# Weight differences of the next unit at products three and four, and token sums begun between the last two row turns

## Chip, cores and metric

The kernel runs on one core of one Trainium2 chip. The metric is the device time of one execution in microseconds. Before the change the median of 3 runs is 3083.6 us (3083.21 to 3086.71).

## What is computed

Two blocks of layers on 512 tokens of width 1024, all in float32. The part that matters here is the gated feed-forward layer, which the second block runs four times, named (l, i) for layer l and place i:

```
def swiglu(x, w_gu, w_down):
    g, u = jnp.split(x @ w_gu, 2, axis=-1)
    return (jax.nn.silu(g) * u) @ w_down

for layer in range(2):
    x = layer_norm(ALPHA * x + 0.5 * swiglu(x, w_gu[layer, 0], w_down[layer, 0]), ...)
    x = layer_norm(ALPHA * x + mixer(x) @ w_out[layer], ...)
    x = layer_norm(ALPHA * x + 0.5 * swiglu(x, w_gu[layer, 1], w_down[layer, 1]), ...)
```

The inner width is 2816: w_gu is 1024 x 5632, w_down is 2816 x 1024.

## The kernel before, in words

**Split operands.** Every product is made from a high part (rounded by a copy on ScalarE) and a low part (the difference to it, a subtraction on VectorE). One 128x128 product is three matmuls: high by high, high by low, low by high (L665 to L667). So each operand costs one ScalarE copy ("high") and one VectorE subtraction ("low"), in that order.

**Units.** The 2816 columns are 11 units of 256. Unit 0 (panels "first") is an ordinary product; each of the units 1 to 10 takes its gate and its up columns by one level of a Strassen-Winograd scheme with FACTORS = 7 products, numbered 0 to 6. A product is 24 matmuls 256 columns wide. Its stationary side is a *factor* of the weights: products 0 and 1 take quarters of the gate panel as they are, product 5 one of the up panel; products 3, 2, 4 and 6 take weight *differences*, which VectorE makes with `difference(u, n)` for n = 3 (L2298), 2 (L2302), 4 (L2304) and 6 (L2308), called d3, d2, d4 and d6 here. Its moving side is the tokens, or one of four token *sums* (sum 1 to 4) made once for each layer by `token_sum(n)` on VectorE (L2265 to L2279), then split by `sum_high` and `sum_low`. Product 2 takes sum 2, product 3 sum 1, product 4 sum 3, product 5 sum 4.

**Buffers.** Two raw panels of 1 MB (RAW[0], RAW[1], "raw" in the rows): the gate panel of a unit in one, the up panel in the other. d3 and d4 are written over raw, d2 into `difference`, d6 into `xt_spare`. Factors go into a ring of 5 slots (w_high, w_low and unit_slot in the rows), so factor q+5 may be written when product q is done.

**Order of the work.** Each engine runs its own list, written by hand as a loop over q (product n of unit u), in order:

- SyncE loads panels in order. The gate panel of unit u+1 waits until factor (u, 3) is ready and d6 of unit u is made; the up panel waits for factor (u, 5).
- ScalarE at step (u, n): copy the bank that product n left ("snapshot", L1753; for products 0, 2, 3 and 4), at n = 2 and 6 a silu, then `high(q + 5)` (L1713): it waits for the panel (n = 0, 1, 5) or the difference.
- VectorE at step (u, n): at n = 1 add for the gate (L2349, `gate_summed`), at n = 5 and 6 the adds and products of the hidden values (L2352 to L2360); at n = 4 d3 and d2 of unit u+1, at n = 6 d4 of unit u+1; then `low(q + 5)` (L2255); at n = 0, after it, d6 of the unit itself. d3 first waits until the up panel has landed.
- TensorE, product n of unit u: waits for its factor, and for n = 2, 4, 5 and 6 until the snapshot of product n-2 is taken:

```
if n in (2, 4, 5, 6):
    pe.wait_ge(sem["snapped"], at("snapped", (f, u, n - 2)))
```

**Ahead of a feed-forward layer** stands `rows(s, y)`: it forms the normed rows tile by tile (4 tiles of 128 tokens), TensorE turns them, ScalarE and VectorE write the high part XTH (L1463) and the low part XTL (L1918) of the turned tokens, and `xt_ready` is given for each tile. The product of unit 0 runs between and behind the turns (`edge_product`); it needs tile 3 only for its second half. Layer (1, 0) has no such turns directly ahead: the key and value products lie between.

## Time and profile before

| What | Value |
|---|---|
| median of 3 runs | 3083.6 us |
| the profiled execution's own time | 3080.08 us |
| its span | 3077.9 us |
| TensorE busy (matmul) | 2904.7 us, 94% |
| TensorE weight loads busy | 2544.3 us, 83% |
| VectorE busy | 1719.4 us, 56% |
| ScalarE busy | 1258.2 us, 41% |
| DMA mean | 91 GB/s |
| mean granted TensorE clock | 0.983 of full |

The profiled execution lies 2.2 us above its span and 3.5 us below the median. TensorE's matmuls are pipelined, so the record of one is longer than the distance to the next; a stretch without a wait shows as fully busy. The page's mean clock hides short stretches at the lower level (0.5 in these units, 1.2 instead of 2.4 GHz). The four unit loops lie at 1074 to 1320 us (0, 0), 1645 to 1891 (0, 1), 2083 to 2334 (1, 0) and 2706 to 2950 (1, 1).

### The profile page before, as it was taken

What the parts mean: (1) busy time and instruction counts of PE and PEld (TensorE: products, weight loads), DVE (VectorE), ACT (ScalarE), POOL (GpSimd) and SP (SyncE); (2) the same over time, 40 slices, a digit from 0 to 9 for tenths busy, and PEclk for the clock granted to TensorE, in tenths of its full rate; (3) what the DMA queues carried; (4) which work ended last, traced back from release to release, by engine and by line L of the source; (5) the groups of instructions that cost most, each with busy time, mean ns of one, the idle gap of its engine ahead of it and who ended that gap; (6) DMA issues with size and microseconds to landing.
All of it is one profiled execution on the core that took longest, in us unless ns stands there. A gap on an engine that the chain in (4) does not pass through costs nothing.

```text
span 3077.9 us, 43267 instructions
## 1 busy us (share of the span) xinstructions
PE 2904.7 (94%) x18236; PEld 2544.3 (83%) x18236; DVE 1719.4 (56%) x2263; ACT 1258.2 (41%) x2081; POOL 101.7 (3%) x153
## 2 busy tenths in 40 slices
PE   7999999999999988899998889997999999989998
PEld 6888887788887878888778888887988876889987
DVE  3464343333336776744668666357665458586653
ACT  3324234444444334433653444224443248444431
POOL 1000000020000000000000000010000011000000
PEclk9999999999999999999999999998999999999999
DMA  5332222222222222233122223351323330212322
GB/s 199 126 109 96 96 96 83 83 77 89 76 79 78 82 83 83 83 123 100 56 69 73 93 83 110 103 146 56 103 89 107 86 97 1 81 57 91 102 103 76
DMA packets 186257, 278.67 MB, mean 91 GB/s; under 512 B 29578, under 2 KB 127034, under 8 KB 185936
## 3 DMA queue, kind: packets, MB, share of 16 engines
q1 hardware_dynamic: 177024, 247.17, 24.8%
q0 software_dynamic: 9040, 28.73, 2.9%
q8 instruction: 145, 2.38, 0.3%
q14 instruction: 48, 0.39, 0.0%
HBM read 271.56 MB, written 4.25 MB: 90 GB/s over the span
## 4 chain that ended last, share of the span: by engine, by line
PE 67%; DVE 15%; issue 7%; ACT 5%; DMA 4%; POOL 0%; SPq 0%; DVEq 0%; ACTq 0%; POOLq 0%
PE bank L665 18%; PE bank L667 18%; PE bank L666 18%; DMA raw<-in_ffn_w_gu 4%; DVE difference L2302 2%; DVE raw L2298 2%; PE bank L803 2%; DVE raw L2304 2%; ACT snapshot L1753 1%; PE bank L891 1%; ACT w_high L1713 1%; PE bank L859 1%; ACT w_low L1713 1%; PE bank L875 1%; PE bank L823 1%
## 5 line engine op out<-in xcount | busy, mean ns | idle before, releaser
L1900 DVE TENSOR_TENSOR w_low<-raw,w_high 128x2048 fp32r<-128x2048 f32 (+1 forms) x132 | 296.1, 2243 | 664.0 <-ACT w_high L1451 658.2
L1451 ACT ACTIVATE w_high<-raw 128x2048 fp32r<-128x2048 f32 (+1 forms) x132 | 247.3, 1874 | 528.3 <-PE bank L667 520.4
L665 PE MATMUL bank<-xt_high,w_high 128*128 128x512 f32 (+1 forms) x1128 | 408.0, 362 | 3.5 <-DVE w_high L2255 2.8
L666 PE MATMUL bank<-xt_low,w_high 128*128 128x512 f32 (+1 forms) x1128 | 399.4, 354 | 0.0
L667 PE MATMUL bank<-xt_high,w_low 128*128 128x512 f32 (+1 forms) x1128 | 399.1, 354 | 0.0
L665 PE MATMUL bank<-w_high,hidden_high 128*128 128x512 f32 x640 | 249.3, 390 | 0.0
L667 PE MATMUL bank<-w_high,hidden_low 128*128 128x512 f32 x640 | 249.0, 389 | 0.0
L666 PE MATMUL bank<-w_low,hidden_high 128*128 128x512 f32 x640 | 249.0, 389 | 0.0
L665 PEld LDWEIGHTS bank<-xt_high,w_high 128*128 128x128 f32 x1128 | 213.7, 189 | 40.4 <-issue 12.5
L667 PEld LDWEIGHTS bank<-xt_high,w_low 128*128 128x128 f32 x1128 | 212.7, 189 | 31.2
L666 PEld LDWEIGHTS bank<-xt_low,w_high 128*128 128x128 f32 x1128 | 213.9, 190 | 27.2
L665 PE MATMUL bank<-sum_high,w_low 128*128 128x256 f32 x512 | 152.8, 298 | 39.9 <-ACT snapshot L1753 39.9
L665 PE MATMUL bank<-sum_high,w_high 128*128 128x256 f32 x512 | 150.6, 294 | 31.6 <-ACT snapshot L1753 30.2
L667 PE MATMUL bank<-sum_high,w_low 128*128 128x256 f32 x512 | 151.1, 295 | 0.0
L666 PE MATMUL bank<-sum_low,w_low 128*128 128x256 f32 x512 | 151.0, 295 | 0.0
L2255 DVE TENSOR_TENSOR w_low<-raw,w_low 128x1024 fp32r<-128x1024 f32 x80 | 98.0, 1225 | 93.8 <-ACT w_low L1713 91.1
L2255 DVE TENSOR_TENSOR w_high<-raw,w_high 128x1024 fp32r<-128x1024 f32 x80 | 98.0, 1225 | 90.3 <-ACT w_high L1713 88.0
L666 PE MATMUL bank<-sum_low,w_high 128*128 128x256 f32 x512 | 148.3, 290 | 0.0
L667 PE MATMUL bank<-sum_high,w_high 128*128 128x256 f32 x512 | 148.2, 289 | 0.0
L666 PEld LDWEIGHTS bank<-w_low,hidden_high 128*128 128x128 f32 x640 | 120.2, 188 | 24.9
L665 PEld LDWEIGHTS bank<-sum_high,w_low 128*128 128x128 f32 x512 | 104.2, 204 | 44.1 <-issue 43.9
L667 PEld LDWEIGHTS bank<-w_high,hidden_low 128*128 128x128 f32 x640 | 120.1, 188 | 24.9
(448 smaller groups left out, 7208.1 us busy)
## 6 DMA issues: line engine op xcount, KB each, us to landing
raw<-in_ffn_w_gu SPq DMA_DIRECT2D x80, 1024.0 KB, 5.8
raw<-in_ffn_w_down SPq DMA_DIRECT2D x44, 1024.0 KB, 4.9
raw<-in_b_w_in SPq DMA_DIRECT2D x40, 1024.0 KB, 5.0
raw<-in_a_w_in SPq DMA_DIRECT2D x24, 1024.0 KB, 5.1
raw<-in_a_w_out SPq DMA_DIRECT2D x8, 1024.0 KB, 4.9
raw<-in_ffn_w_gu SPq DMA_DIRECT2D x16, 512.0 KB, 5.2
raw<-in_w_out SPq DMA_DIRECT2D x5, 1024.0 KB, 4.8
raw<-in_w_mem_kv SPq DMA_DIRECT2D x4, 1024.0 KB, 5.4
```

What stands on the lines that cost most here:

```text
L665: pe.matmul(o, lh, rh, start=start, stop=False, skip_group_check=True)
L666: pe.matmul(o, lh, rl, start=False, stop=False, skip_group_check=True)
L667: return pe.matmul(o, ll, rh, start=False, stop=stop, skip_group_check=True)
L803: ins = pe.matmul(ps[4 + m % 2][:, a:b], q, k, start=True, stop=True)
L823: ins = pe.matmul(ps[7][half:half + 64, x * P:x * P + P], v, PTs[m % 4][:, a:a + P], start=start, stop=stop)
L1451: act.activation(homes[n][0][:, 0:w], RAW[n % 2][:, 0:w], ACT.Copy).then_inc(sem["w_high_ready"], step("w_high_ready", n))
L1713: act.activation(dst, src, ACT.Copy).then_inc(sem["factor_high"], step("factor_high", (f, u, n)))
L1900: dve.tensor_tensor(homes[n][1][:, 0:w], RAW[n % 2][:, 0:w], homes[n][0][:, 0:w].bitcast(F32), ALU.subtract).then_inc(sem["w_low_ready"], ...
L2255: dve.tensor_tensor(dst, src, high.bitcast(F32), ALU.subtract).then_inc(sem["factor_ready"], step("factor_ready", key))
L2298: ins = dve.tensor_tensor(b11, b12, b11, ALU.subtract)
L2302: ins = dve.tensor_tensor(t2, b22, b11, ALU.subtract)
L2304: ins = dve.tensor_tensor(b12, b22, b12, ALU.subtract)
```

## The change

1. **Weight differences.** On VectorE d3 and d2 of unit u+1 move from step n = 4 to n = 3; d6 and d4 of unit u+1 are both made at n = 4, d6 first (before: d4 at n = 6 of unit u, d6 at n = 0 of unit u+1, after that step's low part). Unit 1 keeps d6 at the end of step 0.
2. **Token sums.** Sum 3 and sum 4 begin as high + low of a quarter of the tokens (`join_quarters`), which needs tiles 0 and 1 only. Sum 1 is made in two halves of 128 tokens (`sum_half`), the first of which needs tile 2. In three of the four layers both joins stand between the last rows and the low part of tile 2, and the first half between the low parts of tiles 2 and 3. Sum 2 is then one subtraction (before 2), sum 4 one more (before 3), sum 3 two more (before 3).
3. **First unit.** ScalarE copies sums 1, 2 and 4 ahead of the silus of unit 0. VectorE makes sum 4 ahead of the factors, the low part of factor 2 ahead of the hidden values of unit 0, and at step 0 also the gate's add (before: step 1) and the low part of sum 4 (before: step 1), ahead of factor 5 and d6. `high(5)` stands ahead of sum 3 on ScalarE.

The diff (calls of `rows` left out: those ahead of (0, 0), (0, 1) and (1, 1) get the layer's name as `sums`):

```diff
@@ -1725,16 +1725,17 @@
             high(1)
 
             def sum_high(n):
-                act.wait_ge(sem["sum_ready"], at("sum_ready", (f, n)))
+                act.wait_ge(sem["sum_ready"], at("sum_ready", (f, 1, 1) if n == 1 else (f, n)))
                 act.activation(tiles["sum_high"][n][:], tiles["sum"][n][:],
                                ACT.Copy).then_inc(sem["sum_high"], step("sum_high", (f, n)))
 
+            sum_high(1)
             sum_high(2)
+            sum_high(4)
             for j in range(2):
                 act.wait_ge(sem["product_done"], at("product_done", ("acc", ("first", l, i), j)))
                 act.activation(SNAP[j][:].rearrange("p a n -> p (a n)"), ps[j][:], ACT.Silu).then_inc(sem["gate_read"], step("gate_read", (f, j)))
             high(2)
-            sum_high(1)
             high(3)
             for q in range(count):
                 u, n = 1 + q // FACTORS, q % FACTORS
@@ -1758,13 +1759,11 @@
                 if n == 6:
                     act.activation(GATE2[:].rearrange("p a n -> p (a n)"), A[:],
                                    ACT.Silu).then_inc(sem["unit_gated"], step("unit_gated", (f, u, 1)))
+                if q + 5 < count:
+                    high(q + 5)
                 if q == 0:
                     sum_high(3)
                     high(4)
-                if q == 1:
-                    sum_high(4)
-                if q + 5 < count:
-                    high(q + 5)
                 if u == UNITS - 1:
                     if n == 2:
                         hidden_high(0)
...
@@ -2022,8 +2021,32 @@
             end(2)
             begin(3)
             end(3)
+            if sums:
+                join_quarters(sums, s)
             low(2)
+            if sums:
+                sum_half(sums, s, 0)
             low(3)
+
+        def token_part(high, k0, t0, n=256):
+            return (XTH if high else XTL)[:, k0:k0 + 4, t0:t0 + n].bitcast(F32)
+
+        def join_quarters(f, s):
+
+            dve.wait_ge(sem["xt_ready"], at("xt_ready", (s, 1)))
+            for n, k0 in ((3, 0), (4, 4)):
+                dve.tensor_tensor(FFN[f]["sum"][n][:], token_part(True, k0, 0), token_part(False, k0, 0),
+                                  ALU.add).then_inc(sem["quarter_joined"], step("quarter_joined", (f, n)))
+
+        def sum_half(f, s, h):
+
+            dve.wait_ge(sem["xt_ready"], at("xt_ready", (s, 2 + h)))
+            t0 = 256 + P * h
+            out = FFN[f]["sum"][1][:, :, P * h:P * h + P]
+            link(dve.tensor_tensor(out, token_part(True, 0, t0, P), token_part(True, 4, t0, P), ALU.add))
+            link(dve.tensor_tensor(out, out, token_part(False, 0, t0, P), ALU.add))
+            ins = dve.tensor_tensor(out, out, token_part(False, 4, t0, P), ALU.add)
+            ins.then_inc(sem["sum_ready"], step("sum_ready", (f, 1, h)))
 
         def attend_slot(name, s):
 
@@ -2255,30 +2278,21 @@
                 dve.tensor_tensor(dst, src, high.bitcast(F32),
                                   ALU.subtract).then_inc(sem["factor_ready"], step("factor_ready", key))
 
-            def x(high, k0, t0):
-                return (XTH if high else XTL)[:, k0:k0 + 4, t0:t0 + 256].bitcast(F32)
-
             def token_sum(n):
 
                 out = tiles["sum"][n][:]
-                if n == 1:
-                    link(dve.tensor_tensor(out, x(True, 0, 256), x(True, 4, 256), ALU.add))
-                    link(dve.tensor_tensor(out, out, x(False, 0, 256), ALU.add))
-                    ins = dve.tensor_tensor(out, out, x(False, 4, 256), ALU.add)
                 if n == 2:
-                    link(dve.tensor_tensor(out, tiles["sum"][1][:], x(True, 0, 0), ALU.subtract))
-                    ins = dve.tensor_tensor(out, out, x(False, 0, 0), ALU.subtract)
+                    dve.wait_ge(sem["quarter_joined"], at("quarter_joined", (f, 3)))
+                    dve.wait_ge(sem["sum_ready"], at("sum_ready", (f, 1, 1)))
+                    ins = dve.tensor_tensor(out, tiles["sum"][1][:], tiles["sum"][3][:], ALU.subtract)
+                if n == 4:
+                    dve.wait_ge(sem["quarter_joined"], at("quarter_joined", (f, 4)))
+                    dve.wait_ge(sem["sum_ready"], at("sum_ready", (f, 2)))
+                    ins = dve.tensor_tensor(out, out, tiles["sum"][2][:], ALU.subtract)
                 if n == 3:
-                    link(dve.tensor_tensor(out, x(True, 0, 0), x(True, 0, 256), ALU.subtract))
-                    link(dve.tensor_tensor(out, out, x(False, 0, 0), ALU.add))
-                    ins = dve.tensor_tensor(out, out, x(False, 0, 256), ALU.subtract)
-                if n == 4:
-                    high, low2 = tiles["sum_high"][2][:].bitcast(F32), tiles["sum_low"][2][:].bitcast(F32)
-                    link(dve.tensor_tensor(out, x(True, 4, 0), high, ALU.subtract))
-                    link(dve.tensor_tensor(out, out, x(False, 4, 0), ALU.add))
-                    ins = dve.tensor_tensor(out, out, low2, ALU.subtract)
+                    link(dve.tensor_tensor(out, out, token_part(True, 0, 256), ALU.subtract))
+                    ins = dve.tensor_tensor(out, out, token_part(False, 0, 256), ALU.subtract)
                 ins.then_inc(sem["sum_ready"], step("sum_ready", (f, n)))
-                dve.wait_ge(sem["sum_ready"], at("sum_ready", (f, n)))
 
             def sum_low(n):
                 dve.wait_ge(sem["sum_high"], at("sum_high", (f, n)))
@@ -2315,14 +2329,18 @@
                                   ALU.subtract).then_inc(sem["hidden_split"], step("hidden_split", (f, u)))
 
             prepare(ids["first", l, i][-1])
-            dve.wait_ge(sem["xt_ready"], at("xt_ready", (s, TT - 1)))
-            token_sum(1)
+            if f == (1, 0):
+                join_quarters(f, s)
+                sum_half(f, s, 0)
+            sum_half(f, s, 1)
             token_sum(2)
+            token_sum(4)
             low(0)
             low(1)
             difference(1, 3)
             difference(1, 2)
             sum_low(2)
+            low(2)
             for j in range(2):
                 dve.wait_ge(sem["product_done"], at("product_done", ("acc", ("first", l, i), 2 + j)))
                 dve.wait_ge(sem["gate_read"], at("gate_read", (f, j)))
@@ -2330,10 +2348,9 @@
                 dve.tensor_tensor(tiles["hidden"][0][:, j, :], ps[2 + j][:], SNAP[j][:].rearrange("p a n -> p (a n)"),
                                   ALU.mult).then_inc(sem["up_read"], step("up_read", *labels))
             dve.wait_ge(sem["up_read"], at("up_read", (f, 1)))
-            low(2)
+            token_sum(3)
             sum_low(1)
             low(3)
-            token_sum(3)
             difference(1, 4)
             for q in range(count):
                 u, n = 1 + q // FACTORS, q % FACTORS
@@ -2342,11 +2359,16 @@
                 def bank(b):
                     return b[:].rearrange("p (a n) -> p a n", a=2)
 
-                if n in (1, 5):
-                    dve.wait_ge(sem["unit_done"], at("unit_done", (f, u, n)))
-                if n == 1:
+                def gate_sum():
+
+                    dve.wait_ge(sem["unit_done"], at("unit_done", (f, u, 1)))
                     dve.wait_ge(sem["snapped"], at("snapped", (f, u, 0)))
                     dve.tensor_tensor(SNAP[0][:], bank(B), SNAP[0][:], ALU.add).then_inc(sem["gate_summed"], step("gate_summed", (f, u)))
+
+                if n == 5:
+                    dve.wait_ge(sem["unit_done"], at("unit_done", (f, u, n)))
+                if n == 1 and u > 1:
+                    gate_sum()
                 if n == 5:
                     dve.wait_ge(sem["snapped"], at("snapped", (f, u, 2)))
                     link(dve.tensor_tensor(SNAP[1][:], bank(C), SNAP[1][:], ALU.add))
@@ -2362,20 +2384,19 @@
                 if q == 0:
                     sum_low(3)
                     low(4)
-                    token_sum(4)
-                if q == 1:
+                    gate_sum()
                     sum_low(4)
-                if n == 4 and u + 1 < UNITS:
+                if n == 3 and u + 1 < UNITS:
                     difference(u + 1, 3)
                     difference(u + 1, 2)
-                if n == 6 and u + 1 < UNITS:
+                if n == 4 and u + 1 < UNITS:
+                    difference(u + 1, 6)
                     difference(u + 1, 4)
                 if q + 5 < count:
                     low(q + 5)
-                if n == 0:
-                    if u == 1:
-                        dve.wait_ge(sem["product_done"], at("product_done", ("panel", ids["first", l, i][1])))
-                    difference(u, 6)
+                if q == 0:
+                    dve.wait_ge(sem["product_done"], at("product_done", ("panel", ids["first", l, i][1])))
+                    difference(1, 6)
                 if u == UNITS - 1:
                     if n == 2:
                         hidden_low(0)
...
```

How the lists of VectorE move, at three places. First the turn from one unit to the next, here with unit 3 (L2255 and L2278 are the low parts of factors, L2298, L2302, L2304, L2308 before and L2312, L2316, L2318, L2322 now are d3, d2, d4, d6; numbers behind a name tell buffers apart). Before, on VectorE:

```order
L2298 TENSOR_TENSOR raw_61<-raw_62,raw_61 128x1024
L2302 TENSOR_TENSOR difference_82<-raw_62,raw_61 128x1024
L2255 TENSOR_TENSOR w_low_65<-difference_82,w_low_65 128x1024
L2352 TENSOR_TENSOR snapshot_258<-bank,snapshot_258 128x512
L2354 TENSOR_TENSOR hidden_00_85<-snapshot_258,snapshot_257 128x2x256
L2357 TENSOR_TENSOR snapshot_259<-snapshot_259,snapshot_260 128x512
L2255 TENSOR_TENSOR w_high_64<-raw_61,w_high_64 128x1024
L2360 TENSOR_TENSOR hidden_00_85<-snapshot_259,gate_late 128x2x256
L2304 TENSOR_TENSOR raw_62<-raw_62 128x1024
L2255 TENSOR_TENSOR w_low_66<-raw_62,w_low_66 128x1024
L2255 TENSOR_TENSOR unit_slot_81<-raw_62,unit_slot_81 128x1024
L2308 TENSOR_TENSOR xt_spare_54<-raw_61,difference_82 128x4x256
```

Now, on VectorE at the same place:

```order
L2312 TENSOR_TENSOR raw_61<-raw_62,raw_61 128x1024
L2316 TENSOR_TENSOR difference_82<-raw_62,raw_61 128x1024
L2278 TENSOR_TENSOR w_high_63<-raw_61,w_high_63 128x1024
L2322 TENSOR_TENSOR xt_spare_54<-raw_61,difference_82 128x4x256
L2318 TENSOR_TENSOR raw_62<-raw_62 128x1024
L2278 TENSOR_TENSOR w_low_65<-difference_82,w_low_65 128x1024
L2374 TENSOR_TENSOR snapshot_258<-bank,snapshot_258 128x512
L2376 TENSOR_TENSOR hidden_00_85<-snapshot_258,snapshot_257 128x2x256
L2379 TENSOR_TENSOR snapshot_259<-snapshot_259,snapshot_260 128x512
L2278 TENSOR_TENSOR w_high_64<-raw_61,w_high_64 128x1024
L2382 TENSOR_TENSOR hidden_00_85<-snapshot_259,gate_late 128x2x256
L2278 TENSOR_TENSOR w_low_66<-raw_62,w_low_66 128x1024
```

d6 and d4 now stand directly behind the low part of factor 1, ahead of that of factor 2; d4 no longer stands behind the hidden values, nor d6 at the end.

Second, the last row turns of layer (0, 0) and the start of its feed-forward part (L1918 and L1917 are the low part of the turned tokens; sum_00_74, 71, 77 and 80 are sums 1, 2, 3 and 4). Before, on VectorE:

```order
L1992 TENSOR_TENSOR x_rows<-x_rows,xt_spare_54 128x1024
L1918 TENSOR_TENSOR xt_low<-bank,xt_high 128x4x128 x4
L2265 TENSOR_TENSOR sum_00_74<-xt_high 128x1024
L2266 TENSOR_TENSOR sum_00_74<-sum_00_74,xt_low 128x1024
L2267 TENSOR_TENSOR sum_00_74<-sum_00_74,xt_low 128x1024
L2269 TENSOR_TENSOR sum_00_71<-sum_00_74,xt_high 128x1024
L2270 TENSOR_TENSOR sum_00_71<-sum_00_71,xt_low 128x1024
L2255 TENSOR_TENSOR w_high_63<-raw_61,w_high_63 128x1024
L2255 TENSOR_TENSOR w_low_65<-raw_61,w_low_65 128x1024
L2298 TENSOR_TENSOR raw_61<-raw_62,raw_61 128x1024
L2302 TENSOR_TENSOR difference_82<-raw_62,raw_61 128x1024
L2285 TENSOR_TENSOR sum_low_70<-sum_00_71,sum_high_69 128x1024
```

Now, on VectorE at the same place:

```order
L1991 TENSOR_TENSOR x_rows<-x_rows,xt_spare_54 128x1024
L2038 TENSOR_TENSOR sum_00_77<-xt_high,xt_low 128x1024
L2038 TENSOR_TENSOR sum_00_80<-xt_high,xt_low 128x1024
L1917 TENSOR_TENSOR xt_low<-bank,xt_high 128x4x128 x2
L2046 TENSOR_TENSOR sum_00_74<-xt_high 128x4x128
L2047 TENSOR_TENSOR sum_00_74<-sum_00_74,xt_low 128x4x128
L2048 TENSOR_TENSOR sum_00_74<-sum_00_74,xt_low 128x4x128
L1917 TENSOR_TENSOR xt_low<-bank,xt_high 128x4x128 x2
L2046 TENSOR_TENSOR sum_00_74<-xt_high 128x4x128
L2047 TENSOR_TENSOR sum_00_74<-sum_00_74,xt_low 128x4x128
L2048 TENSOR_TENSOR sum_00_74<-sum_00_74,xt_low 128x4x128
L2287 TENSOR_TENSOR sum_00_71<-sum_00_74,sum_00_77 128x1024
```

The two joins stand ahead of the low part of tile 2 and three adds of half width ahead of that of tile 3.

Third, the first unit of (0, 0), from d4 on. Before, on VectorE:

```order
L2304 TENSOR_TENSOR raw_62<-raw_62 128x1024
L2285 TENSOR_TENSOR sum_low_76<-sum_00_77,sum_high_75 128x1024
L2255 TENSOR_TENSOR unit_slot_81<-raw_62,unit_slot_81 128x1024
L2277 TENSOR_TENSOR sum_00_80<-xt_high,sum_high_69 128x1024
L2278 TENSOR_TENSOR sum_00_80<-sum_00_80,xt_low 128x1024
L2279 TENSOR_TENSOR sum_00_80<-sum_00_80,sum_low_70 128x1024
L2255 TENSOR_TENSOR w_high_63<-raw_62,w_high_63 128x1024
L2308 TENSOR_TENSOR xt_spare_54<-raw_61,difference_82 128x4x256
L2349 TENSOR_TENSOR snapshot_257<-bank,snapshot_257 128x512
L2285 TENSOR_TENSOR sum_low_79<-sum_00_80,sum_high_78 128x1024
```

Now, on VectorE at the same place:

```order
L2318 TENSOR_TENSOR raw_62<-raw_62 128x1024
L2299 TENSOR_TENSOR sum_low_76<-sum_00_77,sum_high_75 128x1024
L2278 TENSOR_TENSOR unit_slot_81<-raw_62,unit_slot_81 128x1024
L2366 TENSOR_TENSOR snapshot_257<-bank,snapshot_257 128x512
L2299 TENSOR_TENSOR sum_low_79<-sum_00_80,sum_high_78 128x1024
L2278 TENSOR_TENSOR w_high_63<-raw_62,w_high_63 128x1024
L2322 TENSOR_TENSOR xt_spare_54<-raw_61,difference_82 128x4x256
L2278 TENSOR_TENSOR w_low_65<-xt_spare_54,w_low_65 128x1024
```

The three subtractions for sum 4 are gone from here; the gate's add and the low part of sum 4 now stand ahead of d6.

## Rows read from the trace of the kernel before

**Rows 1.** Waits of TensorE, whole run: who waited for whom, us in total, times, longest.
```profile
PE bank L665 <- ACT snapshot L1753: 128.3, 61, 11.2
```

**Rows 2.** Windows: stretch, length, busy us of each engine (instructions), PEclk, DMA share, GB/s.
```profile
1099.38:1320.29 220.91, 194.30 (x1560) 191.16 (x1561) 153.85 (x150) 96.47 (x122) 0.00 (x0) 0.98 0.27 89
1670.79:1890.90 220.11, 194.21 (x1561) 191.16 (x1561) 153.84 (x150) 96.48 (x122) 0.00 (x0) 0.98 0.27 88
2112.80:2333.66 220.86, 200.81 (x1561) 198.52 (x1562) 155.38 (x152) 97.02 (x122) 0.00 (x0) 0.95 0.28 91
2731.86:2949.88 218.02, 199.44 (x1562) 197.15 (x1562) 153.86 (x150) 96.91 (x122) 0.00 (x0) 0.95 0.28 89
1154.70:1160.46 5.76, 5.76 (x50) 5.71 (x48) 5.69 (x7) 1.16 (x2) 0.00 (x0) 1.00 0.00 0
```

**Rows 3.** Timeline of VectorE, units 5 and 6: start us, us, [idle before <-releaser].
```profile
1188.28 1.22 DVE L2308 TENSOR_TENSOR xt_spare<-raw,difference 128x1024 f32<-128x1024 f32 x1
1196.07 1.22 DVE L2255 TENSOR_TENSOR w_high<-raw,w_high 128x1024 fp32r<-128x1024 f32 x1 [4.21 <-ACT w_high L1713]
1198.64 1.22 DVE L2298 TENSOR_TENSOR raw<-raw,raw 128x1024 f32<-128x1024 f32 x1
1199.90 1.23 DVE L2302 TENSOR_TENSOR difference<-raw,raw 128x1024 f32<-128x1024 f32 x1
1202.32 1.23 DVE L2255 TENSOR_TENSOR w_high<-difference,w_high 128x1024 fp32r<-128x1024 f32 x1 [1.20 <-ACT w_high L1713]
1205.51 1.23 DVE L2255 TENSOR_TENSOR w_low<-raw,w_low 128x1024 fp32r<-128x1024 f32 x1
1207.25 1.22 DVE L2304 TENSOR_TENSOR raw<-raw 128x1024 f32<-128x1024 f32 x1
1211.03 1.23 DVE L2255 TENSOR_TENSOR w_high<-raw,w_high 128x1024 fp32r<-128x1024 f32 x1
1212.17 1.22 DVE L2308 TENSOR_TENSOR xt_spare<-raw,difference 128x1024 f32<-128x1024 f32 x1
```

**Rows 4.** Timeline of ScalarE in the same stretch.
```profile
1194.98 1.06 ACT L1713 ACTIVATE w_high<-raw 128x1024 fp32r<-128x1024 f32 x1 [3.38 <-DMA raw<-in_ffn_w_gu]
...
1208.51 1.06 ACT L1713 ACTIVATE unit_slot<-raw 128x1024 fp32r<-128x1024 f32 x1 [4.85 <-DVE raw L2304]
```

**Rows 5.** Timeline of TensorE in the same stretch.
```profile
1196.66 0.36 PE L665 MATMUL bank<-sum_high,w_low 128*128 128x256 f32 x1 [1.49 <-ACT snapshot L1753]
...
1210.19 0.36 PE L665 MATMUL bank<-sum_high,w_high 128*128 128x256 f32 x1 [1.78 <-ACT snapshot L1753]
```

**Rows 6.** Timeline of VectorE, row turns and first unit of (0,0).
```profile
1057.04 1.29 DVE L1918 TENSOR_TENSOR xt_low<-bank,xt_high 128x512 fp32r<-128x512 f32 x2 [2.51 <-ACT xt_high L1463]
1060.78 1.29 DVE L1918 TENSOR_TENSOR xt_low<-bank,xt_high 128x512 fp32r<-128x512 f32 x2 [2.45 <-ACT xt_high L1463]
...
1068.40 1.23 DVE L2255 TENSOR_TENSOR w_high<-raw,w_high 128x1024 fp32r<-128x1024 f32 x1
...
1091.28 1.22 DVE L2308 TENSOR_TENSOR xt_spare<-raw,difference 128x1024 f32<-128x1024 f32 x1
```

**Rows 7.** Timeline of VectorE, row turns ahead of (0,1).
```profile
1626.26 1.29 DVE L2003 SCALAR_TENSOR_TENSOR x_rows<-x_rows,small,gain 128x1024 f32<-128x1024 f32 x1 [0.67 <-POOL small L2580]
1628.27 1.29 DVE L1918 TENSOR_TENSOR xt_low<-bank,xt_high 128x512 fp32r<-128x512 f32 x2 [0.73 <-ACT xt_high L1463]
1632.01 1.29 DVE L1918 TENSOR_TENSOR xt_low<-bank,xt_high 128x512 fp32r<-128x512 f32 x2 [2.45 <-ACT xt_high L1463]
```

**Rows 8.** Timeline of VectorE, first unit of (1,0).
```profile
2081.74 1.23 DVE L2255 TENSOR_TENSOR w_high<-raw,w_high 128x1024 fp32r<-128x1024 f32 x1 [18.83 <-ACT w_high L1713]
...
2104.63 1.22 DVE L2308 TENSOR_TENSOR xt_spare<-raw,difference 128x1024 f32<-128x1024 f32 x1
```

**Rows 9.** Timeline of VectorE in (1,0): both panels asked for after the first row.
```profile
2128.35 1.22 DVE L2308 TENSOR_TENSOR xt_spare<-raw,difference 128x1024 f32<-128x1024 f32 x1
...
2139.00 1.23 DVE L2298 TENSOR_TENSOR raw<-raw,raw 128x1024 f32<-128x1024 f32 x1 [0.40 <-DMA raw<-in_ffn_w_gu]
```

10 lines of the change are left out of this document (5 added, 5 removed).

## Prediction

> **What bounds the kernel now.** I read three views in this order. First the waits of TensorE: nearly all its idle time is one line, 128.3 us in 61 waits [rows 1], all inside the unit loops of the four feed-forward layers. The releaser named, the snapshot, need not be the cause: it is the last link of a longer chain. Second, windows over each loop from product 5 of unit 1 to the start of the down product, 65 products each: 220.91, 220.11, 220.86 and 218.02 us, together 879.90 [rows 2]. The last window holds two products without a wait: 5.76 us for 48 matmuls, 0.12 us a matmul, so 2.88 a product and 20.16 us a unit. 65 products need 187.2 us, four loops 748.8. Thus 131.1 us lie there in waits and in matmuls at the lower clock. The clock belongs in it: the last two loops have a mean granted clock of 0.95 and fewer waits than the first two at 0.98, with nearly the same length [rows 2], as they would if something other than TensorE set the pace.
>
> Third, the timelines show what. On VectorE d6 of unit 5 starts at 1188.28 and d6 of unit 6 at 1212.17: a turn of 23.89 us against TensorE's 20.16 [rows 3]. The turn is one closed chain. d6 frees the raw gate panel; the next one lands and ScalarE takes it at 1194.98, 5.5 us after d6 ended [rows 4]; the low part follows at 1196.07, a second one, d3 at 1198.64, d2, then 1.20 us of waiting for ScalarE's copy of d2, the hidden values, d4 at 1207.25, again a wait for ScalarE's copy, the low part of factor 5 and d6 [rows 3]. TensorE waits twice in a turn, though no factor is late. ScalarE's next snapshot is queued behind a copy. For product 5 (1.49 us [rows 5]) that is the copy waiting for the panel, for product 2 (1.78 us) the copy waiting 4.85 us for d4 [rows 4].
>
> **The unit loop after the change.** d6 of unit u+1 is now made at product 4 of unit u, so the gate panel is held by the low part of factor 3 alone. I follow the new turn from the landing of the up panel, which d3 needs, with distances from rows 3:
> - d3 to d2 1.26, d2 to low part 1 1.25 (d2 is waited for), low part to d6 1.14 (as 1211.03 to 1212.17), d6 to d4 and d4 to low part 2 1.25 each: 6.15.
> - Low part 2 to low part 3 with the hidden values between, 1202.32 to 1205.51: 3.19.
> - Low part 3 to 4: the slot that d4 has today, 1205.51 to 1207.25: 1.74. Low part 4 to 5: 1.14. Low part 5 itself: 1.23, and the up panel is asked for.
>
> That is 13.45 us. ScalarE's copies of d2 and d4 are now covered by d6 and other low parts. To it comes the transfer. Where both panels are asked for together, at the end of d6 at 2129.57, d3 waits until 2139.00: the second lands 9.4 us after [rows 9]. The gate panel is now asked for 1.74 + 1.14 = 2.9 us earlier than the up panel, which then lands 6.5 us after its own request, if the pair still takes 9.4. The turn is 13.45 + 6.5 = 19.95 us, under 20.16. Thus TensorE becomes the bound, narrowly. A small overshoot costs little: when unit 2 begins, VectorE is by my ledger some 2 us ahead of product 2, and only what adds up over eight turns beyond that is paid.
>
> ScalarE's snapshots: d4 is made before product 0, so the copy of factor 4 no longer holds the one for product 2. The gate panel is asked for at about the end of product 6, lands 5.5 us later, and its copy is due at the end of product 2, 3 × 2.88 = 8.6 us later: 3 us to spare. Both waits go; with no waits the clock stays up. What is late next is nothing on the list; VectorE's 13.45 us plus a panel is. The down product behind the loop waits for no copy that the change moves. I cost the loops at their 748.8 us: **−131.1**.
>
> The size of this term can be read in two ways. The rows show TensorE busy for 194.30 + 194.21 + 200.81 + 199.44 = 788.76 of the 879.90 us, which leaves 91.1 idle [rows 2]. By that column −91.1 would be all there is, and the end 2978 us. I take 131.1, since 48 matmuls in 5.76 us [rows 2] is a rate and slow matmuls count as busy. The Trainium skill's page "Perfetto Trace Analysis" (Identifying the Most-Contended Engine) says that the busy share of matmuls is not a good measure of the distance to the limit; by that rule the 2978 falls away.
>
> **The first unit.** Product 4 of unit 1 waits longest (up to 11.2 us [rows 1]): ScalarE's snapshot for it stands behind the copy of d6, and d6 behind all token sums on VectorE. After it the second gate panel is asked for, which fixes product 5. So both, and all behind, move with the end of d6. In (0, 0) VectorE runs without a pause from tile 3's low part to d6's end at 1092.50 [rows 6]. Linked full operations take 1.25 [rows 3]; those of half width I take at 0.72, from 1.29 for the pair in an xt_low row [rows 6] and a link. Removed: 11 sum operations, 13.75. Put in their place: three halves 2.16 and four full ones 5.0. Moved ahead of d6: the gate's add 0.61 and a low part 1.14. Together −13.75 + 7.16 + 1.75 = **−4.8**.
> The joins and the first half must hide in the row turns. In (0, 0) VectorE waits 2.51 and 2.45 us there [rows 6], against 2.4 for the joins and 2.1 for the half: free. Ahead of (0, 1) the first gap is 0.73 [rows 7]: joins from 1627.46 (1.2 after the rows' start) put tile 2's low part at 1629.74, and the half then puts tile 3's at 1633.11 instead of 1632.01. 1.1 us of d6's gain are lost, **−3.7**; TensorE may wait 0.7 us for tile 3, which costs nothing since product 4 waits for d6 anyway. (1, 1) has the same pattern: **−3.7**. In (1, 0) the sums are ready long before, VectorE waits 18.83 us for a copy [rows 8]; only sums 3 and 4 shorten the stretch (−5.0 + 1.75), and two copies more stand ahead of the silus, 1.9 us on ScalarE, of which low part 2 sees about 1.2: **−2.0**. Together −14.2.
>
> **Sum.** −131.1 − 14.2 = −145.3 against the profiled execution's 3080.1: 2934.8. The median lies 3.5 us higher; I predict **2938 us** for the median. Nothing is added elsewhere: transfers are the same in number and size, and VectorE's sums are 12 instructions a layer for 11, six of them of half width.
>
> **Rivals.**
> - *A, the panels set the pace.* The turn's margin is 0.2 us and rests on one distance. If the up panel lands 9.4 us after its own request (the longest wait rows show), the turn is 22.85. Eight turns of 2.7 too much, less 2 of advance, are 19.6 a layer, 78 in all: 3016. With 7.5 us the turn is 20.95, 4 a layer, 17 in all: 2955. For it: both panels share one queue. Against: a panel asked for alone is there in 5.5 [rows 3, 4], and the gate panel has a start of 2.9. Chance of A near its far end 0.10; its near end lies in the forecast's case. The Trainium skill's page "DMA: Bandwidth & Descriptors" (Bandwidth) has 1 MB occupy the engines for 6.15 us; an estimate by it is over 12 us for a pair and an end near A's. By that rule the trace does not agree: the pair took 9.4 in all [rows 9].
> - *B, it does only half of what it says.* The wait for product 5 stays because the gate panel's request, held by low part 3, is not early enough; only the wait for product 2 goes. 1.49 us over nine units and four layers are 54 us: 2992. Chance 0.06.
> - *C, slower.* d3 waits for the up panel, and it now stands one step earlier, ahead of d6, d4 and low parts 1 and 2 on VectorE's in-order list. From a landing more than 10.4 us after the request the turn exceeds today's 23.89. At 11.5 us each turn is 25.0, 1.1 × 36 = 40 us more, less 14: 3110. No row has such a landing. Chance 0.02. With it no change at all, 0.02.
>
> **Numbers.** Forecast 0.80, A 0.10, B 0.06, slower 0.02, same 0.02 (0.2%, 6 us, is about what a measurement of this kernel can tell from no change). The forecast's own bounds: the loops can give no more than their 131.1, and the first units give more only as d6 ends earlier; with my ledger of VectorE 4 us a layer too long the end is 2922. Upwards it reaches 2955 with late panels. The range goes on from there towards B, to the 2978 that the busy column gives: 2922 to 2978, with 0.20 left out. Faster 0.96.
>
> **What would show it.** Windows between the first units and the down products at 187 to 189 us each, clock 1.00 from unit 2 on; TensorE's waits fall from 128 to some 25 us, about 4 to 7 for each product 4 of unit 1 and some 2 for its product 5; VectorE's idle time before low part 5, released by ScalarE, which waits for TensorE; no wait of ScalarE for d4. d6 of unit 1 in (0, 0) ends near 1087.7. Wrong would be a turn of VectorE above 20.5 us with d3 released by the panel (A), or a wait of 1.2 to 1.5 us left before each product 5 (B).

## Result and profile after

| | Before | After |
|---|---|---|
| median | 3085.15 us (4 runs) | 2935.41 us (2934.14 to 2937.16, 4 runs) |
| the profiled execution's own time | 3080.08 us | 2937.16 us |
| its span | 3077.9 us | 2935.3 us |
| TensorE busy | 2904.7 us, 94% | 2866.2 us, 98% |
| mean granted clock | 0.983 | 0.994 |

The median before has one more run than at the time of the prediction. The ratio to the kernel before is 0.9514, 95% interval [0.9498, 0.9531]. The forecast was 2938 us for the median. Its sum, 2934.8 us for the profiled execution, is 2.4 us under the measured 2937.16.

The waits of TensorE, whole run, in the changed kernel: who waited for whom, us in total, times, longest.

```profile
PE bank L665 <- issue: 21.2, 8, 6.0
PE bank L784 <- DVE row L1938: 20.5, 6, 9.5
PE bank L665 <- DVE w_high L2278: 2.8, 1, 2.8
```

The 128.3 us for the snapshot [rows 1] are gone. Eight waits at the same line are left, now named "issue", all in unit 1. Four stand before product 4 (3.65, 3.76, 6.02 and 3.75 us) and three before product 5 (0.71, 1.26 and 0.68); these have the old cause under another name. The eighth, 1.35 us before product 2 of layer (1, 0), is new: there the kernel before had no wait. It costs nothing by itself, since product 4 of that layer waits for d6 anyway.

Windows over the four loops, from product 5 of unit 1 to the down product, against [rows 2] (columns as there).

```profile
1095.10:1282.57 187.47, 187.47 (x1560) 187.47 (x1561) 154.85 (x152) 99.41 (x122) 0.00 (x0) 1.00 0.33 107
1629.08:1816.34 187.26, 187.26 (x1561) 187.26 (x1561) 154.85 (x152) 99.79 (x122) 0.00 (x0) 1.00 0.33 107
2036.96:2224.23 187.27, 187.27 (x1560) 187.27 (x1561) 155.13 (x152) 99.55 (x122) 0.00 (x0) 1.00 0.33 107
2620.00:2807.27 187.27, 187.27 (x1560) 187.27 (x1561) 155.13 (x152) 99.56 (x122) 0.00 (x0) 1.00 0.33 107
```

The busy column of TensorE equals the length in each, and the clock is 1.00: no product waits. Together 749.27 us for 879.90, **130.6 us less**. The other 12.0 us of the span lie ahead of the loops: from one loop to the next product 5 the changed kernel is 4.3, 4.0, 1.3 and 2.4 us shorter, and behind the last loop nothing moved (128.02 and 128.03 us).

The timeline of VectorE in a settled stretch, from the end of one turn to the start of the next, against [rows 3].

```profile
1207.89 0.69 DVE L2366 TENSOR_TENSOR snapshot<-bank,snapshot 128x512 f32<-128x512 f32 x1
1209.05 1.23 DVE L2278 TENSOR_TENSOR w_low<-xt_spare,w_low 128x1024 fp32r<-128x1024 f32 x1 [0.46 <-ACT w_low L1713]
1212.87 1.22 DVE L2278 TENSOR_TENSOR unit_slot<-raw,unit_slot 128x1024 fp32r<-128x1024 f32 x1 [2.59 <-ACT unit_slot L1713]
1214.19 1.23 DVE L2312 TENSOR_TENSOR raw<-raw,raw 128x1024 f32<-128x1024 f32 x1
1215.45 1.22 DVE L2316 TENSOR_TENSOR difference<-raw,raw 128x1024 f32<-128x1024 f32 x1
1216.71 1.22 DVE L2278 TENSOR_TENSOR w_high<-raw,w_high 128x1024 fp32r<-128x1024 f32 x1
1217.86 1.22 DVE L2322 TENSOR_TENSOR xt_spare<-raw,difference 128x1024 f32<-128x1024 f32 x1
1219.11 1.23 DVE L2318 TENSOR_TENSOR raw<-raw 128x1024 f32<-128x1024 f32 x1
...
1234.36 1.23 DVE L2312 TENSOR_TENSOR raw<-raw,raw 128x1024 f32<-128x1024 f32 x1
```

d3 (L2312) comes 20.17 us after the one before, at TensorE's pace. In this stretch it waits for nothing; VectorE idles one step earlier, for ScalarE, whose copy waits until TensorE has freed a slot of the ring. That is what a kernel bound by TensorE looks like on VectorE.

The timeline of VectorE, ScalarE and TensorE in the first unit of (0, 0), against [rows 6].

```profile
1057.35 1.29 DVE L1917 TENSOR_TENSOR xt_low<-bank,xt_high 128x512 fp32r<-128x512 f32 x2 [0.24 <-ACT xt_high L1463]
1061.09 1.29 DVE L1917 TENSOR_TENSOR xt_low<-bank,xt_high 128x512 fp32r<-128x512 f32 x2 [0.27 <-ACT xt_high L1463]
...
1086.59 1.22 DVE L2322 TENSOR_TENSOR xt_spare<-raw,difference 128x1024 f32<-128x1024 f32 x1
```

```profile
1087.85 1.06 ACT L1713 ACTIVATE w_low<-xt_spare 128x1024 fp32r<-128x1024 f32 x1 [5.34 <-DVE xt_spare L2322]
1088.81 0.58 ACT L1754 ACTIVATE snapshot<-bank 128x512 f32<-128x512 f32 x1
```

```profile
1089.49 0.56 PE L665 MATMUL bank<-sum_high,unit_slot 128*128 128x256 f32 x1 [3.65 <-issue]
```

The waits of 2.51 and 2.45 us in the row turns are down to 0.24 and 0.27: joins and half sum fill them. d6 ends at 1087.81 (forecast 1087.7); its copy, the snapshot behind it and product 4 follow in a chain, as before.

### The profile page after: what moved, and what is told of

It is laid out like the page before. It is cut to its first block, busy times and chain, and to the rows that moved or that the text cites. A ratio compares the mean times of both kernels' runs of the same rounds, so it can differ in the third digit from the quotient of the medians.

```text
span 2935.3 us, 43271 instructions
## 1 busy us (share of the span) xinstructions
PE 2866.2 (98%) x18236; PEld 2515.3 (86%) x18236; DVE 1708.3 (58%) x2267; ACT 1269.1 (43%) x2081; POOL 101.4 (3%) x153
## 4 chain that ended last, share of the span: by engine, by line
PE 88%; DVE 7%; issue 2%; ACT 2%; DMA 1%; POOL 0%; SPq 0%; POOLq 0%; DVEq 0%; ACTq 0%
PE bank L665 25%; PE bank L667 25%; PE bank L666 25%; PE bank L803 2%; PE bank L891 1%; PE bank L859 1%; PE bank L875 1%; PE bank L823 1%; PE bank L812 1%; PE bank L676 1%; PE bank L679 1%; PE bank L678 1%; PE bank L784 1%; DVE sum_low L2299 1%; PE bank L1037 0%
## 5 line engine op out<-in xcount | busy, mean ns | idle before, releaser
L1754 ACT ACTIVATE snapshot<-bank 128x512 f32<-128x512 f32 x160 | 95.3, 596 | 182.3 <-PE bank L667 172.7
L665 PE MATMUL bank<-sum_high,w_high 128*128 128x256 f32 x512 | 145.4, 284 | 4.1 <-issue 4.0
L665 PE MATMUL bank<-sum_high,w_low 128*128 128x256 f32 x512 | 145.0, 283 | 0.9 <-DVE w_low L2278 0.9
L666 PE MATMUL bank<-sum_low,w_low 128*128 128x256 f32 x512 | 144.9, 283 | 0.0
L667 PE MATMUL bank<-sum_high,w_low 128*128 128x256 f32 x512 | 144.9, 283 | 0.0
L667 PE MATMUL bank<-sum_high,w_high 128*128 128x256 f32 x512 | 144.9, 283 | 0.0
L665 PEld LDWEIGHTS bank<-w_high,hidden_high 128*128 128x128 f32 x640 | 120.1, 188 | 24.8
L665 PE MATMUL bank<-w_high,xt_high 128*128 128x512 f32 (+1 forms) x336 | 130.2, 388 | 0.0
```

What stands on the lines that cost most here:

```text
L665: pe.matmul(o, lh, rh, start=start, stop=False, skip_group_check=True)
L666: pe.matmul(o, lh, rl, start=False, stop=False, skip_group_check=True)
L667: return pe.matmul(o, ll, rh, start=False, stop=stop, skip_group_check=True)
L1754: act.activation(SNAP[to][:].rearrange("p a n -> p (a n)"), bank[:], ACT.Copy).then_inc(sem["snapped"], step("snapped", (f, u, n)))
```

## Experiments

All kernels ran beside the kernel before on the same chip (its medians there were 3081.3 to 3083.8 us). "Window" is from product 5 of unit 1 to the down product.

### The two parts apart

`differences_alone` is the kernel before with this edit, `sums_alone` the changed kernel with its reverse:

```diff
-                if n == 4 and u + 1 < UNITS:
+                if n == 3 and u + 1 < UNITS:
                     difference(u + 1, 3)
                     difference(u + 1, 2)
-                if n == 6 and u + 1 < UNITS:
+                if n == 4 and u + 1 < UNITS:
+                    difference(u + 1, 6)
                     difference(u + 1, 4)
...
-                if n == 0:
+                if q == 0:
...
-                    difference(u, 6)
+                    difference(1, 6)
```

> The kernel before with the new places of the weight differences in the unit loop (d3, d2 at product 3; d6, d4 at product 4), token sums and first unit as they were. The turn theory (a closed chain over VectorE and the panels set 23.9 us a unit) gives the loops back whole, as in the changed kernel: about 130 us off 3085, so 2955, with the waits of up to 11 us at product 4 of unit 1 still there. A rival, that loops and sums help only together, would leave a turn above 20.5 us in this kernel and an end above 2975.

> The changed kernel with the weight differences at their old places; the token sums and the first unit as changed. The turn theory: windows of about 220 us between the first units and the down products as before, and only the first units' 12 us gained: 3073. If the late start of VectorE in the first unit was what kept the loop behind, the windows would be shorter too and the end under 3050.

Measured: `differences_alone` 2950.97 us, ratio 0.9577 [0.9563, 0.9592]; `sums_alone` 3067.21 us, ratio 0.9955 [0.994, 0.997]. That is 131.0 and 14.7 us less than before on their chip, 145.7 together; the whole change is worth 149.7 by its medians and 142.6 by the spans of the two profiled executions. Three of the four windows of `sums_alone`:

```profile
1095.32:1315.13 219.81, 196.37 (x1561) 193.65 (x1561) 154.00 (x150) 96.78 (x122) 0.00 (x0) 0.97 0.27 89
1661.59:1882.57 220.98, 199.95 (x1562) 197.16 (x1561) 153.80 (x150) 96.87 (x122) 0.00 (x0) 0.95 0.27 88
2102.16:2322.86 220.70, 192.61 (x1561) 189.60 (x1561) 154.09 (x150) 96.33 (x122) 0.00 (x0) 0.99 0.27 88
```

The fourth is 218.93 us long. The loops keep their length although their first units are as short as in the changed kernel. The parts do not need each other. These rows also show what the clock is worth here: at 0.99 and at 0.95 the window is 220.7 and 221.0 us. A faster TensorE only waits longer: in these windows its clock has no price of its own, since VectorE's turn sets the pace.

### d4 or d6 alone

```diff
                 if n == 4 and u + 1 < UNITS:
                     difference(u + 1, 3)
                     difference(u + 1, 2)
+                    difference(u + 1, 4)
```

This is `d4_early_alone` (d6 as before, at the end of step 0). In `d6_early_alone` the added line is `difference(u + 1, 6)`, and d4 stays at n == 6. Both have the token sums and the first unit of the changed kernel.

> The changed kernel, with d3, d2 and then d4 at product 4 and d6 at its old place, at the end of step 0 of its own unit. The turn theory: d4's own slot (1.25 us) and the wait for ScalarE's copy of it (1.2 us) leave the chain, but d6 still frees the gate panel, so the turn falls from 23.9 to about 21.4, the wait before product 5 stays, and the end is some 2985. The rival, that each wait of TensorE stands for itself, gives back just the 1.78 us before product 2, 64 us in all beside the 12: about 3009.

> The changed kernel, with d3, d2 and then d6 at product 4 and d4 at its old place, behind the hidden values of product 6. The turn theory: the gate panel is no longer freed by the last step of the chain, the turn of VectorE is about 20.0 us, so d4 is no longer late and the snapshot for product 2 comes in time although its place on ScalarE is the old one: 2935 to 2950. The rival, that each wait stands for itself, keeps the 1.78 us before product 2, 64 us: about 3000.

Measured: d4 early 2973.72 us, ratio 0.965 [0.9634, 0.9666]; d6 early 2952.32 us, ratio 0.9583 [0.9569, 0.9598]. One window of each (65 products):

```profile
1095.47:1292.83 197.36, 189.04 (x1561) 187.65 (x1561) 153.47 (x151) 96.22 (x122) 0.00 (x0) 1.00 0.30 99
```

```profile
1094.91:1286.16 191.25, 189.28 (x1561) 187.72 (x1561) 154.46 (x152) 97.87 (x122) 0.00 (x0) 1.00 0.32 105
```

With d4 early d3 comes every 21.42 us on average (1097.49 to 1268.83 in eight turns), as the turn theory had it (21.4). The end is 11 us under the expected 2985, which does not follow from that turn: (21.4 - 20.16) × 8 turns × 4 layers are 40 us on top of the changed kernel, 2975. The waits before product 2 are gone and one before product 5 is left in nearly each unit:

```profile
PE bank L665 <- ACT snapshot L1754: 28.8, 31, 2.6
```

With d6 early it comes every 20.39 us (1096.93 to 1260.04), 0.4 more than the ledger's 20.0, and the end is 2 us above the expected 2935 to 2950. Why the turn is 20.39 was not followed further. VectorE still waits 1.2 us a turn for ScalarE's copy of d4, but of that only some 0.2 us a unit reaches TensorE. The rival, that each wait is a loss by itself, wanted 3009 and 3000 and falls. The two gains overlap: the four windows add up to 786.3 us with d4 early (93.6 less than before), 767.9 with d6 early (112.0 less) and 749.3 with both (130.6 less). Either step shortens the same turn, and the second is worth only what is left above 20.16.

What d6 does in the old order shows on SyncE's queue. Its waits in the first window of the kernel before:

```profile
SPq L645 <- DVE xt_spare L2308: 205.8, 9, 24.3
SPq L654 <- DVE w_low L1900: 8.4, 1, 8.4
```

and in that of the changed kernel:

```profile
SPq L645 <- DVE xt_spare L2322: 97.8, 9, 12.3
SPq L654 <- DVE w_high L2278: 30.5, 7, 5.7
SPq L654 <- DVE w_low L2278: 27.6, 7, 5.7
SPq L654 <- DVE unit_slot L2278: 16.7, 4, 5.7
```

Before, the up panel's request never waited for a factor: each of the nine pairs was asked for at once when d6 was done. Now the gate panel goes when low part 3 is done and the up panel when low part 5 is, 18 waits of their own.

### d3 and d2 back at product 4

`d3_at_product_four`: in the changed kernel `difference(u + 1, 3)` and `difference(u + 1, 2)` stand at n == 4, ahead of d6 and d4.

> The changed kernel with all four differences at product 4, d3 and d2 one step later than in the change, behind the low part of factor 1. Now TensorE bounds the loop and VectorE waits some 3 us a turn, so one place costs nothing: 2935, within 5 us. The rival, that the move of d3 and d2 to product 3 carries part of the gain, gives windows over 190 us and an end above 2950.

Measured: 2935.6 us, ratio 0.952 [0.9504, 0.9536], the same as the change. Moving d3 and d2 to product 3 is worth nothing here: in either order VectorE waits in each turn for ScalarE's copies ahead of d3 (0.46 + 2.59 us in the changed kernel, 3.25 + 0.48 us in this one), and what is gained goes into these waits.

### How much margin the turn has

```diff
                 if n == 2:
...
+                    for again in range(2 if u > 1 else 0):
+                        link(dve.tensor_tensor(t2, b22, b11, ALU.subtract))
                     ins = dve.tensor_tensor(t2, b22, b11, ALU.subtract)
```

(`two_more_subtractions`; `one_more_subtraction` has range(1).)

> The changed kernel with d2 made twice in units 2 to 10, one more linked subtraction of 1.25 us on VectorE in each turn. In the changed kernel VectorE's own turn, where it still catches up, is 18.7 us (d3 of unit 4 at 1155.7, of unit 5 at 1174.4), so with one more it is 19.97, still under TensorE's 20.16: under 4 us more than 2935. By the prediction's ledger (19.95 without it) it would be 21.2, one us too long in each of eight turns: some 25 to 35 us more.

> The same with d2 made three times, two more linked subtractions in each turn. By the 18.7 us read from the changed kernel the turn is 21.2: 1.06 us too long over eight turns, less what VectorE is ahead by then (about 3 us), 5 to 8 us a layer, 20 to 30 us more than 2935. By the prediction's ledger (22.45) 2.3 too long, 16 to 18 a layer: about 65 to 75 more.

Measured: 2950.5 us with one (ratio 0.9569 [0.9554, 0.9583]), 15 more than the change; 2998.0 us with two (0.9724 [0.971, 0.9739]), 63 more. Both lie between the expectations: the margin is larger than the prediction's 0.2 us and smaller than the 1.4 that I read from one pair of rows of the changed kernel. The starts of d3 with two more subtractions, where VectorE sets the pace, show why:

```profile
1117.46 1.23 DVE L2312 TENSOR_TENSOR raw<-raw,raw 128x1024 f32<-128x1024 f32 x1 [0.66 <-DMA raw<-in_ffn_w_gu]
...
1140.20 1.23 DVE L2312 TENSOR_TENSOR raw<-raw,raw 128x1024 f32<-128x1024 f32 x1 [1.83 <-DMA raw<-in_ffn_w_gu]
...
1161.40 1.23 DVE L2312 TENSOR_TENSOR raw<-raw,raw 128x1024 f32<-128x1024 f32 x1 [0.63 <-DMA raw<-in_ffn_w_gu]
...
1182.62 1.23 DVE L2312 TENSOR_TENSOR raw<-raw,raw 128x1024 f32<-128x1024 f32 x1 [0.59 <-DMA raw<-in_ffn_w_gu]
...
1205.02 1.22 DVE L2312 TENSOR_TENSOR raw<-raw,raw 128x1024 f32<-128x1024 f32 x1 [1.83 <-DMA raw<-in_ffn_w_gu]
...
1226.27 1.22 DVE L2312 TENSOR_TENSOR raw<-raw,raw 128x1024 f32<-128x1024 f32 x1 [0.60 <-DMA raw<-in_ffn_w_gu]
```

The distances are 22.74, 21.20, 21.22, 22.40 and 21.25 us: in two of these five turns the up panel is 1.2 to 1.5 us late. Over the eight turns of this loop the mean is (1269.72 - 1096.16) / 8 = 21.70, over the four loops 21.84 (21.70, 21.88, 22.00 and 21.79); without the two additions (2.51) that is 19.3. With one more subtraction the mean of the four loops is 20.57, less 1.25 again 19.3. The margin of the changed kernel is thus 20.16 - 19.3 = **0.8 us a turn**. One more subtraction of 1.25 overruns it by 0.4, two by 1.7; in eight turns of four layers that is 13 and 54 us. The four windows are together 15.3 and 60.9 us longer than those of the changed kernel; the rest of 2 and 7 us was not followed further.

VectorE's idle time would have misled: it idles 3.3 us a turn in the changed kernel (0.22 + 0.46 + 2.59), and an addition of 1.25 still costs time. The chain runs through the landing of the up panel: VectorE may be idle there, but the chain is not.

### Sums behind the turns

`sums_behind_the_turns` leaves `join_quarters` and the first `sum_half` out of `rows` and puts them where (1, 0) has them, for all layers:

```diff
-            if sums:
-                join_quarters(sums, s)
             low(2)
-            if sums:
-                sum_half(sums, s, 0)
             low(3)
...
-            if f == (1, 0):
-                join_quarters(f, s)
-                sum_half(f, s, 0)
+            join_quarters(f, s)
+            sum_half(f, s, 0)
```

> The changed kernel with both joins and the first half of sum 1 behind the row turns in every layer, as it has them in (1, 0) alone; the work is the same. If they hid in the turns and d6 of unit 1 follows all of VectorE's list, d6 comes 4.6 us later in (0, 0) and 3.5 in (0, 1) and (1, 1): 11 to 12 us more than 2935. If product 4 of unit 1 does not hang on d6, under 3 more.

Measured: 2945.72 us, ratio 0.9553 [0.9539, 0.9567]; 10.3 more than the change. From the start of unit 1 to its product 5 the three layers take 25.11, 24.78 and 24.74 us instead of 20.94, 20.75 and 20.55; (1, 0), untouched, takes 27.37 and 27.82. The windows behind are the same to 0.3 us. So some 10 us of what sums and first unit give are the work hidden in the row turns.

### What the waits left in the first unit are worth

Waits of 3.7 to 6.0 us at product 4 and of up to 1.3 at product 5 are left, and the matmuls of product 4 behind such a wait run at a lower clock: granted 0.50 in (0, 0), 0.63, 0.67 and 0.66 in the other three layers. `snapshots_first` tries to take them by turning ScalarE's list in unit 1:

```diff
+                if q in (3, 4):
+                    high(q + 3)
-                if q + 5 < count:
+                if q + 5 < count and q not in (1, 2):
                     high(q + 5)
```

> The changed kernel with one piece of ScalarE's list turned in the first unit: the copy of d6 stands behind the snapshot of product 3, and the copies of factors 0 and 1 of unit 2 behind that of product 4; VectorE is untouched. If product 4 of unit 1 hangs on d6 only by ScalarE's order, its wait (3.7 us in three layers, 6.0 in (1, 0)) and that of product 5 go; what is late next is the low part of d2 of unit 2 on VectorE, ready at 1103.7 in (0, 0) where product 2 now starts at 1106.9: 3 us a layer, so some 2923. If the wait is VectorE's own (low part of factor 4 or of sum 3 late), nothing moves: 2935.

Measured: 2936.28 us, ratio 0.9533 [0.952, 0.9546]. The edit did not do what its expectation says: at q == 3 the copy of factor 1 of unit 2 came out ahead of the snapshot of product 4, so product 6 of unit 1 waits in its place, 3.2 us in (0, 0) (it starts at 1094.82; without the wait it would be 1091.45). `snapshots_first_again` has at q == 3 only the copy of d6, and at q == 4 those of factors 0 and 1 of unit 2.

> What the first of the two kernels with the snapshots first was meant to be: the copy of factor 1 of unit 2 too now stands behind the snapshot of product 4 (there it stood ahead, so that product 6 waited for the panel). Products 4, 5 and 6 of unit 1 should follow without a wait. But both earlier runs show the next link: the snapshot of product 0 of unit 2 overwrites what the hidden values of unit 1 read, and these stand behind six subtractions on VectorE, at 1105.0 in that run. So if VectorE's list is what counts, product 2 of unit 2 starts at about 1106.5 whatever TensorE saves before it: 2935, within 2 us. If the waits seen at products 4 and 5 were time lost in full, it would be some 2915.

Measured: 2937.62 us, ratio 0.9536 [0.9523, 0.9549]. In (0, 0) products 4, 5 and 6 of unit 1 follow without a wait and product 6 starts at 1091.72 instead of 1098.25, 6.5 us earlier. Waits before products 0, 1 and 2 of unit 2 (0.87, 1.24 and 2.62 us) and matmuls at the lower clock take nearly all of it back; product 2 starts 1.1 us earlier than in the changed kernel:

```profile
1105.77 0.38 PE L665 MATMUL bank<-sum_high,unit_slot 128*128 128x256 f32 x1 [2.62 <-ACT snapshot L1754]
```

On ScalarE that snapshot waited for the hidden values of unit 1 on VectorE, which stand behind d3, d2, d6, d4 and two low parts:

```profile
1105.02 0.60 ACT L1754 ACTIVATE snapshot<-bank 128x512 f32<-128x512 f32 x1 [1.59 <-DVE hidden L2381]
```

So the 6.5 us could not be had in this way: VectorE's list, not the wait that TensorE shows, fixes when unit 2 can go on. `d6_first_in_unit_one` therefore moves the work on VectorE:

```diff
                 if q == 0:
+                    dve.wait_ge(sem["product_done"], at("product_done", ("panel", ids["first", l, i][1])))
+                    difference(1, 6)
                     sum_low(3)
                     low(4)
...
+                if q == 3:
+                    high(7)
-                if q + 5 < count:
+                if q + 5 < count and q != 2:
                     high(q + 5)
```

> The changed kernel with d6 of unit 1 made directly behind d4 on VectorE, ahead of the low parts of sum 3 and factor 4, 5 us earlier, and on ScalarE the copy of factor 0 of unit 2 behind the snapshot of product 3. The gate panel of unit 2 is then asked for 5 us earlier and TensorE's waits at products 4 and 5 of unit 1 go; the low part of d2 of unit 2 comes at about 1101, one us late: 5 to 6 us a layer, so some 2913. If the up panel, asked for behind the low part of factor 5, is what fixes unit 2, it is no better than the kernel with the snapshots first, some 2923.

Measured: **2925.97 us** (2923.09 to 2926.24), ratio 0.9495 [0.9482, 0.9508], 10.3 less than `snapshots_first`, which ran beside it. In (0, 0) products 4 to 6 of unit 1 and 0 of unit 2 run without a wait, the latter at 1094.44 instead of 1101.13 (in (1, 0) product 4 still waits 1.65 us). Of these 6.7 us 2.6 are lost again before product 2 of unit 2 and 1.5 at the lower clock in it: some 2.5 us a layer are left of the 5 to 6 expected.

`hidden_values_early` goes after that wait: for unit 1 the hidden values of product 5 stand ahead of d3 and d2, and the low part of factor 2 of unit 2 ahead of d6 and d4.

```diff
-                if n == 5:
-                    dve.wait_ge(sem["unit_done"], at("unit_done", (f, u, n)))
...
-                if n == 5:
+                if q == 3 or n == 5 and u > 1:
+                    dve.wait_ge(sem["unit_done"], at("unit_done", (f, u, 5)))
...
+                if q == 4:
+                    low(9)
                 if n == 4 and u + 1 < UNITS:
```

> The kernel with d6 first in unit 1, and two more moves on VectorE for unit 1 alone: its hidden values of product 5 stand ahead of d3 and d2 of unit 2, in the 2.9 us in which d3 waits for the up panel, and the low part of factor 2 of unit 2 stands ahead of d6 and d4. If the snapshot that follows the hidden values is what held product 2 of unit 2 (2.6 us in each layer, then 1.5 us at the lower clock), both go and the next bound is the low part of factor 2 near 1099: 3 to 4 us a layer, some 2912. If that wait is the low part itself, under 4 us are gained: 2922 or more.

Measured: 2924.9 us (2922.02 to 2925.62), ratio 0.9489 [0.9476, 0.9502], not to be told from the kernel before it. The expectation's first theory, 2912, is wrong; the number fits the second, but not for its reason, since the wait is still the snapshot's and not the low part's. ScalarE's rows show the link that took over:

```profile
1101.14 1.06 ACT L1713 ACTIVATE w_low<-raw 128x1024 fp32r<-128x1024 f32 x1 [2.30 <-DVE raw L2320]
1102.10 0.58 ACT L1754 ACTIVATE snapshot<-bank 128x512 f32<-128x512 f32 x1
```

The snapshot no longer waits for the hidden values but stands behind the copy of d4, and d4 was pushed back by what was put ahead of it, from 1098.13 to 1099.88. The snapshot comes at 1102.10, where it came at 1102.04. The next step would be to let that snapshot pass the copy of d4; it was not tried.

## Why the prediction was right, step by step

- **The loops, -131.1.** Measured -130.6. The clock was in it as forecast: the busy column alone would have given -91.1. The Trainium skill's page "Perfetto Trace Analysis" (Identifying the Most-Contended Engine) offers, beside the arithmetic rate, the busy share of weight loads in the place of matmuls; by that column of [rows 2] (777.99 of 879.90) it would have been -101.9, which the runs contradict as well. Weight loads too last longer at the lower clock: 25 of them were busy 5.20 us at clock 0.50 (1089.49 to 1095.10 in the changed kernel) and 2.88 us at 1.00 (1107.22 to 1110.10 in `hidden_values_early`).
- **VectorE's turn, 13.45 + 6.5 = 19.95.** The first number holds to 0.02 us: in the changed kernel d3 of one unit starts at 1155.71 and low part 5 ends at 1169.18, 13.47 later. The second was the term mis-sized. Where VectorE sets the pace (`two_more_subtractions`), d3 starts 5.9 us after low part 5 ends, on average over four loops, so the turn is 19.3 and the margin 0.8 instead of 0.2. The prediction also called the 5.5 us of [rows 3, 4] those of a panel asked for alone; they are those of the first of a pair. Neither moved the forecast, since the turn stays under 20.16 either way. Rival A depended on it: its far end needed 9.4.
- **"At about the end of product 6" the gate panel is asked for, and both snapshot waits go.** Right; no wait is left in any window.
- **First units, -4.8, -3.7, -2.0, -3.7.** Measured -4.3, -4.0, -1.3, -2.4. Between the start of unit 1 and its product 5 they are -4.6, -5.0, -1.9 and -5.1; on the other side the units 1 start 0.3, 1.0, 0.6 and 2.6 us later. In (0, 1) and (1, 1) 0.7 and 0.75 of that is the wait for tile 3 that the prediction named and put at nothing, because product 4 waits for d6 anyway. The last layer falls short most, and 1.6 us of it came from an attention stage that the change does not touch: from 2413.09 to 2417.00 the granted clock was 0.56, while the same matmuls before (2522.52 to 2524.97) ran at 1.00, behind the same two waits of 1.04 and 0.71 us. That comes and goes from one profile to the next, in a stage that all these kernels share: from the end of the loop before to unit 1 of (1, 1) the changed kernel takes 375.2 us, as do the profiles of `sums_alone`, `d4_early_alone`, `d6_first_in_unit_one` and `hidden_values_early`, but those of the six other kernels with the joins in the row turns take 373.6.
- **The step from the profile to the median.** The prediction added 3.5 us, because the profiled execution before was that far below its median. After the change it is 1.8 us above its median. So the sum was 2.4 us too low and the step 5.2 too high; that the forecast ends 2.6 us from the measured 2935.41 is in part luck.
- **Rival B (product 5's wait stays).** Not seen: low part 3 ends 5.7 us behind d6 and SyncE asks for the gate panel then, and that was early enough.
- **Rival C (d3 late, slower).** Its price was real in kind: `two_more_subtractions` has d3 released by the panel in each turn. Its point, a landing 10.4 us after the request, was never near.
- **Signatures.** Windows 187.3 to 187.5 us and a clock of 1.00 as forecast. The waits left are 21.2 us, forecast some 25: 17.2 for product 4 (3.7 us in three layers, 6.0 in one, forecast 4 to 7), but only 2.7 for product 5 (forecast some 2 each), and 1.35 before product 2 of (1, 0), which was not among the signatures. VectorE's idle time is released by ScalarE, as said, but it stands ahead of low part 0 (2.6 us), not ahead of low part 5.

## What to carry to other kernels

When a trace shows many small waits at the same places of a loop, look for a closed chain over several engines that comes round once in each pass, and compare its turn with the pace that the waiting engine could keep by itself: here 23.9 against 20.16. Steps taken out of that chain are worth the difference once, however many waits they end; two steps that shorten the same chain do not add up. The idle time of an engine is not its margin either. And taking a wait away is worth nothing if the list of another engine fixes a later point: taking the waits of 4 to 6 us at product 4 away changed nothing until VectorE's own work was moved.
